# A second key buffer, level-one products in four array quarters, modulation sums without a total, and half the forward spectra

## The reference

```python
mod = silu(c) @ ada_w[layer] + ada_b[layer]              # shift, scale, gate rows
# RWKV-7, 16 heads of 64, context then latent tokens, both directions z
k_dir = k * (1 + (a - 1) * k_a);  b = kk * a             # a = sigmoid(a0 + low rank)
S = S * w_t + (S @ a_t) b_t^T + v_t k_t^T;  y_t = S @ r_t
# Hyena, order 2
z = x1 * fft_conv(v, kern[0]);  y = x2 * fft_conv(z, kern[1])
# experts: top-1 group, top-2 experts of 32
y_e = (silu(x @ w_gate[e]) * (x @ w_up[e])) @ w_down[e]
```

## Time and profile before

| | |
|---|---|
| median of 3 runs | 1964.73 us (1961.82 to 1973.62) |
| profiled execution | 1960.14 us |
| its span in the trace | 1958.2 us |
| mean granted clock of TensorE | 0.969 |
| PE, PEld, DVE, ACT, POOL busy | 1776.7, 941.9, 773.4, 531.2, 52.1 us |
| chain steps, first to last copy of U | 149.8 to 702.9 us |
| convolutions | 1355.7 us to about 1450 us |

### The profile page before, as it was taken

One profiled execution on the slowest core, in us unless ns is written; L12 is line 12 of the kernel. 1 busy time (PEld: TensorE's weight loads), 2 busy tenths in 40 slices (PEclk: granted clock), 3 DMA queues, 4 the chain that ended last, 5 costly groups with the idle time before them and its releaser, 6 DMA issues. The chain is left out here.

```text
span 1958.2 us, 34257 instructions
## 1 busy us (share of the span) xinstructions
PE 1776.7 (91%) x13979; PEld 941.9 (48%) x13979; DVE 773.4 (39%) x1910; ACT 531.2 (27%) x993; POOL 52.1 (3%) x45
## 2 busy tenths in 40 slices
PE   5788898898897888999999999898999999999996
PEld 2344555555555544443443443675654444444442
DVE  5766677777777335200100101564735110110101
ACT  3244454554454321111111111213321111111111
POOL 0010000000100000000000001000000000000001
PEclk8989899999999899999999999999999999999998
DMA  9013323323323468999999997232166999999993
GB/s 308 26 33 101 99 73 114 114 77 111 110 76 127 162 238 360 427 428 428 428 429 428 428 416 277 76 128 112 82 272 272 427 428 428 428 428 428 428 413 123
DMA packets 105168, 504.05 MB, mean 257 GB/s; under 512 B 15568, under 2 KB 60352, under 8 KB 79184
## 3 DMA queue, kind: packets, MB, share of 16 engines
q1 hardware_dynamic: 103728, 501.88, 64.4%
q10 hardware_dynamic: 1312, 0.37, 0.1%
HBM read 501.13 MB, written 1.09 MB: 256 GB/s over the span
## 5 line engine op out<-in xcount | busy, mean ns | idle before, releaser
L2009 DVE TENSOR_TENSOR arena<-banks,arena 128x512 f32<-128x512 f32 x32 | 22.1, 692 | 660.5 <-PE banks L1821 660.5
L1821 PE MATMUL banks<-arena 128*64 128x512 f32 x1024 | 226.4, 594 | 10.5 <-DMA arena<-in_moe_w_up 10.5
L1843 PE MATMUL banks<-arena 128*64 128x512 f32 x1024 | 226.8, 596 | 3.3 <-ACT arena L1940 3.3
L1812 PE MATMUL banks<-arena 128*64 128x512 f32 x1024 | 225.3, 593 | 3.3 <-DVE arena L1932 3.3
L775 PE MATMUL banks<-arena 128*128 128x512 f32 (+1 forms) x384 | 159.3, 553 | 0.8 <-ACT arena L1086 0.8
L1821 PEld LDWEIGHTS banks<-arena 128*64 128x64 f32 x1024 | 82.1, 137 | 152.8 <-issue 152.8
L1812 PEld LDWEIGHTS banks<-arena 128*64 128x64 f32 x1024 | 74.2, 137 | 147.8 <-issue 144.2
L1843 PEld LDWEIGHTS banks<-arena 128*64 128x64 f32 x1024 | 70.7, 137 | 154.4 <-issue 150.7
L1934 ACT ACTIVATE arena<-banks,arena 128x128 f32<-128x128 f32 x128 | 48.1, 456 | 335.5 <-PE banks L1801 335.5
L1801 PEld LDWEIGHTS banks<-arena 128*128 128x128 f32 x1024 | 118.4, 194 | 28.1 <-issue 24.3
L1801 PE MATMUL banks<-arena 128*128 128x128 f32 x1024 | 124.5, 281 | 3.5 <-DVE arena L2004 3.5
(11 more groups left out here) (394 smaller groups left out, 2398.0 us busy)
## 6 DMA issues: line engine op xcount, KB each, us to landing
arena<-in_moe_w_gate SPq DMA_DIRECT2D x64, 2048.0 KB, 14.9
arena<-in_moe_w_up SPq DMA_DIRECT2D x64, 2048.0 KB, 17.1
arena<-in_moe_w_down SPq DMA_DIRECT2D x64, 2048.0 KB, 12.8
arena<-in_ada_w SPq DMA_DIRECT2D x128, 192.0 KB, 2.9
...
```

Source lines behind the costliest of these rows:

```text
L1812: mm = pe.matmul(G[j * CAP:(j + 1) * CAP, :], xT[:, t, j * CAP:(j + 1) * CAP], wg[par][j][:, t], start=(t == 0), stop=(t == KT - 1))
L1821: mm = pe.matmul(U[j * CAP:(j + 1) * CAP, :], xT[:, t, j * CAP:(j + 1) * CAP], wu[j][:, t], start=(t == 0), stop=(t == KT - 1))
L1843: mm = pe.matmul(bank[j * CAP:(j + 1) * CAP, :], hT[:, t, j * CAP:(j + 1) * CAP], wd[j][:, t, half * 512:(half + 1) * 512], start=(t == 0) ...
L2009: dve.tensor_tensor(h, U[:, :], sg, ALU.mult).then_inc(h_ready, 1)
```

## The change

Seven things change.

1. There are two key buffers, KK[n % 2]. key_rates, key_products and rates of group q = m + 2 move to slots 20, 22 and 23 of the round before, the sum and the features are spread over slots 0, 1, 3 and 4, and products_early goes from slot 6 to 5, kept_early from 7 to 6. factors is cut into inner_factors (slot 21 of the round before) and outer_factors (z = 0 in slot 22 of the round before, z = 1 in slot 1).
2. level_one makes both results together, in four quarters: for each block s1 in its own partition half and s2 in the other (z swapped); level_two_z and level_two follow with the half of z2 and s2 exchanged.
3. The modulation's four weight tiles are summed in PSUM. Each product is made in four column groups of a quarter of the piece's width, so 16 products stand in place of four; the total, its copy and ACT's store go. DVE's second sum writes the row, on four partitions, and SP stores it ahead of the next bias. The modulation's places in open_order and the slots change (h0 in slot 2, h1 in 7; the products a after h4, the products w in slot 14).
4. A pair of low rank products takes both banks before the first product.
5. sum_directions alternates between its two outputs.
6. ACT does a Sigmoid on one spare word in slot 11, and decay_rank moves to slot 14.
7. In the convolutions only the first block of each forward spectrum's matrix is used: the products of even and odd tokens are kept apart, ACT copies one of them, and DVE makes sum and difference as the two blocks.

The diff, cut:

```diff
+    def part(self, piece):
+
+        return self.width(piece) // 4
+
+    def store(self, sp, m, piece, open_dve):
+
+        layer, cols = self.place(m, piece)
+        sp.wait_ge(open_dve, OPEN.taken(m, f"h{2 * piece + 1}")[1])
+        sp.dma_start(self.mods[layer, 0, cols].rearrange("(g n) -> g n", g=4),
+                     self.row[0:P:32, 0:self.part(piece)]).then_inc(self.row_out, 16)
...
-            if half == 0:
-                sp.wait_ge(open_dve, OPEN.taken(*before)[1])
         if half == 0:
-            sp.dma_start(self.bias[0:1, 0:self.width(piece)], self.ins["ada_b"][layer, cols].unsqueeze(0)).then_inc(self.bias_in, 16)
+            if m or k:
+                self.store(sp, *((m, piece - 1) if piece else (m - 1, self.PIECES - 1)), open_dve)
+            sp.dma_start(self.bias[0:P:32, 0:self.part(piece)],
+                         self.ins["ada_b"][layer, cols].rearrange("(g n) -> g n", g=4)).then_inc(self.bias_in, 16)
...
-        for g in range(self.HALF):
-            mm = pe.matmul(bank[g * 32:(g + 1) * 32, 0:self.width(piece)], self.cond[:, half * self.HALF + g],
-                           self.w[g][:, 0:self.width(piece)], start=True, stop=True, tile_position=(0, g * 32))
+        n = self.part(piece)
+        for t in range(self.HALF):
+            for g in range(4):
+                mm = pe.matmul(bank[g * 32:(g + 1) * 32, 0:n], self.cond[:, half * self.HALF + t],
+                               self.w[t][:, g * n:(g + 1) * n], start=(t == 0), stop=(t == self.HALF - 1), tile_position=(0, g * 32))
         return mm
...
-        order += [(m, u) for u in ("wy0", "wy1", "h0") if chain]
-        order += [(m, u) for u in ("h1", "t0") if chain]
+        order += [(m, u) for u in ("h0", "wy0", "wy1") if chain]
+        order += [(m, u) for u in ("h1",) if chain]
         order += [(m + 1, u) for u in ("v",) if now]
         order += [(m, u) for u in ("h2",) if chain]
         order += [(m + 1, u) for u in ("bc", "kc", "vc") if now]
         order += [(m - 1, u) for u in ("rows",) if behind]
-        order += [(m + 2, u) for u in ("w0", "w1") if early]
+        order += [(m + 1, u) for u in ("wyc",) if now]
         order += [(m, u) for u in ("h3",) if chain]
-        order += [(m + 1, u) for u in ("wyc",) if now]
-        order += [(m, u) for u in ("t1",) if chain]
-        order += [(m + 2, u) for u in ("k", "a0", "a1") if early]
+        order += [(m + 2, u) for u in ("w0", "w1", "k") if early]
         order += [(m, u) for u in ("h4",) if chain]
+        order += [(m + 2, u) for u in ("a0", "a1") if early]
         order += [(m + 2, u) for u in ("norm",) if early]
         order += [(m, u) for u in ("h5",) if chain]
         order += [(m + 2, u) for u in ("rg",) if early]
-        order += [(m, u) for u in ("t2",) if chain]
...
-    BB, KK = [s.take(STEPS, 2, C) for _ in range(2)], s.take(STEPS, 2, C)
+    BB, KK = [s.take(STEPS, 2, C) for _ in range(2)], [s.take(STEPS, 2, C) for _ in range(2)]
...
-                    if slot == 2 and 0 <= n and n + 1 < CH:
+                    if slot == 4 and 0 <= n and n + 1 < CH:
                         sp.wait_ge(open_done, OPEN.done(n, "rg"))
                         r.load_first(sp, ins, n + 1)
                     if slot == 13 and 0 <= n and n + 1 < CH:
                         sp.wait_ge(open_done, OPEN.done(n, "v"))
                         r.load_values(sp, ins, n + 1)
-                    if 0 <= m < CH and slot in (4, 8, 12, 15, 19):
-                        later.load(sp, m, (4, 8, 12, 15, 19).index(slot) + 1, open_done, open_dve)
+                    if 0 <= m < CH and slot in (3, 8, 12, 15, 19):
...
-                if name == "w0":
+                if name == "w":
                     pe.wait_ge(kr_in, 96 * (n + 1))
-                z = int(name[1])
-                w, x = (w2, r.wl) if name[0] == "w" else (a2, r.al)
-                pe.matmul(open_bank(n, name)[:, :], w[rows(z), :], x[rows(z), :], start=True, stop=True).then_inc(open_done, 1)
+                w, x = (w2, r.wl) if name == "w" else (a2, r.al)
+                banks = [open_bank(n, f"{name}{z}") for z in range(2)]
+                for z in range(2):
+                    pe.matmul(banks[z][:, :], w[rows(z), :], x[rows(z), :], start=True, stop=True).then_inc(open_done, 1)
...
-                level(n, "s1" + "cl"[half], lambda z, b: S2[:, half, b], lambda z, b: z1[:, b])
-                level(n, "s2" + "cl"[half], lambda z, b: z1[:, b], lambda z, b: S2[:, half, b])
+                first, second = (inverse_bank(n, k + "cl"[half]) for k in ("s1", "s2"))
+                for b in range(BLK):
+                    at = slice(b * C, (b + 1) * C)
+                    s2_, z_ = S2[:, half, b], z1[:, b]
+                    pe.matmul(first[rows(0), at], s2_[rows(0)], z_[rows(0)], start=True, stop=True)
+                    pe.matmul(second[rows(0), at], z_[rows(1)], s2_[rows(1)], start=True, stop=True)
+                    last_first = pe.matmul(first[rows(1), at], s2_[rows(1)], z_[rows(1)], start=True, stop=True)
+                    last_second = pe.matmul(second[rows(1), at], z_[rows(0)], s2_[rows(0)], start=True, stop=True)
+                last_first.then_inc(inv_done, 1)
+                last_second.then_inc(inv_done, 1)
...
                     if chain and slot == 2:
                         level_one_z(m, 1)
+                        modulate(m, 0)
                         from_values_late(m, 0)
                     if chain and slot == 3:
                         from_values_late(m, 1)
-                        modulate(m, 0)
                     if chain and slot == 4:
                         level_one(m, 1)
+                    if now and slot == 5:
+                        products_early(n)
                     if chain and slot == 6:
+                        level_two_z(m, 1)
+                    if chain and slot == 7:
                         modulate(m, 1)
-                    if now and slot == 6:
-                        products_early(n)
-                    if chain and slot == 7:
-                        level_two_z(m, 1)
                     if now and 7 <= slot < 9:
                         products_late(n, slot - 7)
                     if chain and slot == 8:
-                        total(m, 0)
                         level_two(m, 1)
                     if now and 9 <= slot < 12:
                         project(n, "v", ((0, 1, 2), (3, 4, 5), (6, 7))[slot - 9])
                         modulate(m, 2)
                     if now and slot == 12:
                         turn(n, "bc", BB[n % 2], 0)
-                        turn(n, "kc", KK, 0)
+                        turn(n, "kc", KK[n % 2], 0)
                     if now and slot == 13:
                         turn(n, "vc", VV, 0)
                     if behind and slot == 13:
                         out_rows(m - 1)
-                    if early and slot == 13:
-                        low_rank(q, "w0")
-                        low_rank(q, "w1")
+                    if now and slot == 14:
+                        from_values_early(n)
                     if chain and slot == 14:
                         modulate(m, 3)
-                    if now and slot == 14:
-                        from_values_early(n)
-                    if chain and slot == 15:
-                        total(m, 1)
+                    if early and slot == 14:
+                        low_rank(q, "w")
                     if early and 15 <= slot < 18:
                         project(q, "k", ((0, 1), (2, 3, 4), (5, 6, 7))[slot - 15])
-                    if early and slot == 18:
-                        low_rank(q, "a0")
-                        low_rank(q, "a1")
                     if now and slot == 18:
                         level_one_z(n, 0)
                     if chain and slot == 18:
                         modulate(m, 4)
+                    if early and slot == 18:
+                        low_rank(q, "a")
...
-            def factors(n, z):
+            def inner_factors(n, z):
                 act.wait_ge(dec_ready, 2 * n + z + 1)
                 inner, sign = (sg[z], -1.0) if z == 0 else (cum[z], 1.0)
-                outer = cum[z] if z == 0 else sg[z]
+                act.activation(inner, inner, ACT.Exp, scale=sign * HALF_DECAY)
...
+            def outer_factors(n, z):
+                outer, sign = (cum[z], -1.0) if z == 0 else (sg[z], 1.0)
                 to = late(n % 2, z, 1)
+                if z == 0 and n >= 2:
+                    act.wait_ge(g_done, STEPS * (n - 1))
                 act.activation(to, outer[:, L:TOK].rearrange("p (j t) -> p j t", t=C), ACT.Exp, scale=sign * HALF_DECAY)
-                act.activation(inner, inner, ACT.Exp, scale=sign * HALF_DECAY)
                 act.drain()
                 act.activation(outer, outer, ACT.Exp, scale=-sign * HALF_DECAY)
...
-                    if now and slot == 1:
-                        factors(n, 0)
                     if chain and slot == 1:
```

(72 more changed lines are left out.)

97 lines of the change are left out of this document (43 added, 54 removed).

## The result

The changed kernel takes 1947.1 us (median of 6 runs, 1942.6 to 1950.0) beside 1966.5 us for the kernel before (6 runs in the same session, 1960.8 to 1973.6): a ratio of 0.990, with an interval of 0.988 to 0.992. The forecast was 1900, with a range from 1874 to 1934. The sign was right, the size was not: 1.0% came of 3.3%.

A forecast was written before the change was run, and what follows sets the result against it. The prediction took PE to lead the head rounds with DVE close behind, a chain of eight steps setting each round. Heads 54.5 us and convolutions 6 us off the profiled 1960.14 gave 1900, range 1874 to 1934.

The forecast's parts named there:

- Step 0: First to second copy of U in a round: 8.01 to 6.8 us, ACT's exponentials and the wait before L877 gone.
- Step 4: Fifth to sixth copy of U: 10.77 to 10.6 us, w products waiting 2.3 to 2.6 for the h3 sum.
- Step 5: Sixth to seventh copy of U: 10.80 to 10.1 us, a products 0.6 shorter but waiting 0.4 for h4.
- Step 3: Fourth to fifth copy of U: 8.21 to 8.3 us, with the sigmoid's table load ahead of the turned tiles' copies.
- Steps 1, 2, 6 and 7: Other steps between copies of U in a round: 5.4, 9.1, 7.2 and 8.1 us forecast.
- Level one: Two level-one results together in four quarters: 0.9 us less per pair, 16 pairs, 14.5 us.
- The modulation products and totals: Head rounds: totals removed save 2.4 us a round, 19 in all; modulation products in column groups cost PE no change.
- The third rival: Slower: short modulation products' weight loads do not overlap, 2.7 us more a group, 130 us, giving 2030; chance 0.04.
- The convolutions: Convolution stage: halved forward and inverse products against added DVE operations, 6 us saved.
- the fast side: Head rounds: PE stalls vanish rather than move, 24 us more saved over seven rounds, giving 1876; chance 0.12.
- a slow side: DVE becomes the bound wherever its work was moved, a saving of only 30 us, giving 1930; chance 0.17.
- 1900 and its surroundings: Whole kernel: the main forecast, 1884 to 1918 us; chance 0.62.

The follow-up runs named there:

- e1: The changed kernel with modulation product h0 put back behind both late value products, in bank order and slot 3: 1929.5 us, ratio 0.985.
- e2: The changed kernel with the low rank products of w and their sigmoids put back ahead of modulation product h3: 1933.1 us, ratio 0.986.
- e3: The changed kernel with both orders put back, h0 behind the late value products and w with its sigmoids ahead of h3: 1913.9 us, ratio 0.976.
- e10: The kernel before with only the modulation change: four column groups, no totals, store on SP; orders, slots and key buffer as before: 1948.4 us, ratio 0.994.
- e8: e3 with the two low rank products of the rates put ahead of modulation product h4, in bank order and on PE: 1917.4 us, ratio 0.977.
- e9: e3 without the early sigmoid on a spare word, so the table load stands later again: 1924.6 us, ratio 0.981.
- e5: The kernel before with only level one in four array quarters and the swapped halves in level two: 1963.8 us, ratio 1.0006.
- e4: e3 with level one written again as two levels of two quarters, one after the other: 1916.6 us, ratio 0.977.
- e6: The kernel before with only the convolution change, products of even and odd halves with sum and difference on DVE: 1962.0 us, ratio 1.0004.

## Why the forecast missed, point by point

By the profiled executions 60.5 us were to go and 16.9 went. Of the 43.6 missing, about 28.6 are in the first six rounds, 8.4 in the last two, 4.4 in the opening and 2.3 behind the rounds.

- **Step 0 (forecast 6.8, came 8.6).** This is a wait that was left out, not a mis-sized one. The forecast said that the wait before L877 goes and stopped there. It never asked who holds the bank of wy1 once h0 stands ahead in the ring. The diff shows the order; DVE's slot 3, level copy before `modulate(m, 0)`, was in the text of the kernel. e1 shows 2.0 us a round.
- **Step 4 (10.6, came 12.7).** The mechanism was named, the w products waiting for h3, and e2 shows it to be the cause. Its size was wrong: 2.3 to 2.6 us were laid out, 3.35 came, and the work behind it is slower as well. The low rank pair then takes 1.71 us in step 4, and four records of the same kind 1.1 in step 5. The windows view has the granted clock at 0.50 for 3.4 us behind the wait, at 0.62 over the pair, and at 1.00 in step 5:

```profile
402.70:406.10 3.40, 3.27 (x22) 1.34 (x19) 1.40 (x4) 1.42 (x3) 0.00 (x0) 0.50 0.31 80
402.30:404.00 1.70, 1.70 (x8) 0.36 (x11) 0.00 (x0) 0.56 (x2) 0.00 (x0) 0.62 0.06 11
416.60:417.70 1.10, 1.08 (x6) 0.34 (x6) 0.95 (x5) 0.00 (x0) 0.00 (x0) 1.00 0.35 102
```

  So the lower clock that follows the long wait adds 0.6 us to the pair and some 1.6 to the step, and the forecast's sum left it out: e3's step of 8.83 us has 1.58 of waits, its other 7.25 and the wait of 3.35 make 10.6, and this one took 12.2.
- **Step 5 (10.1, came 11.1).** The forecast had 0.4 us of wait for h4, and the changed kernel has 0.54. So the wait does not explain the miss, and e10 has 11.2 here without any moved bank use. What makes this step longer with the shorter modulation products was not found. In e3 the wait grows to about 1.1, since PE comes to it sooner; e8 shows that it is worth 1.0 us in this step and can't be had for nothing.
- **Step 3 (8.3, came 8.8).** The early table load costs 0.5, not 0.1, of step 3. e9 shows what it saves: 2.8 us of step 4 in e3's order. The edit that looks like a cost is one of the useful ones.
- **Steps 1, 2, 6 and 7 (29.8, came 29.8).** These hold in sum and nearly one by one: 5.4, 9.6, 6.6, 8.2 against 5.4, 9.1, 7.2, 8.1. Step 1 is partly luck: it would be 4.7, as in e1 and e3, without the "issue" waits, whose cause is open. The stall for DVE before the state product, 25.0 us in the earlier trace rows, is gone from the first six rounds, and the solve waits for DVE's sum in step 6 as forecast, 1.25 us for the 1.5 laid out.
- **Level one (14.5; by the medians nothing in e5, 3 in e4).** The price was right and the place was not. The 64 instructions run from 372.69 to 373.63 in the changed kernel, some 1.1 with the last one's end, 0.8 less than the 1.9 read from the earlier trace rows. But what PE waits for next ends later than either form: DVE's features in step 1 (0.41 against 1.17) and DVE's sum in step 6 (0.48 against 1.26). The forecast took 0.9 off two steps because PE leads the round; it did not look at what PE waits for next behind this group.
- **The modulation products and totals (19, came 14.4).** The price was right: 1536 instructions take 48.1 us, a group 1.08 at 128 columns and 0.80 to 0.87 at 96, in the changed kernel. Their lines:

```profile
L253 PE MATMUL banks<-arena 128*32 128x96 f32 (+1 forms) x1536 | 48.1, 265 | 9.0 <-DMA arena<-in_ada_w 5.3 <-issue 3.7
L253 PEld LDWEIGHTS banks<-arena 128*32 128x32 f32 x1536 | 36.0, 112 | 18.2 <-issue 15.9
```

  The 1536 loads of 112 ns cover 36.0 us, 23 ns apiece, as in the earlier trace rows. The third rival at 2030 is out. The rule of the Trainium skill (TensorE: Matmul & The Clock Gate, Part 3, The mechanism), by which these loads would not overlap, does not describe them. The Trainium skill (TensorEngine Tiling (Array Packing), Key Properties) has different tiles loading and multiplying at once, and with that this trace agrees, at 23 ns for a load of 112.
- **The moves around the second key buffer.** No term of the sum stood for them alone, and they turned out to be the largest part. From e10's 1948.4 to e4's 1916.6 lie 31.8 us; e4 has all of e3 but level one, so this is the moved work with both orders put back, with the low rank pairs, the early table load and about 3 us of convolutions in it. No run has the key buffer alone.
- **The rounds counted.** Seven rounds at the full saving and 3.5 us more for the last were laid out. Round 6 has no work for the next round but one, so fewer of the stalls that could go. The last two rounds took 112.7 us before and 110.3 after: 2.4 us for the forecast's 10.8. In e3 they give 7.3. This stretch varies by itself: it takes 114.4 us in e6, whose rounds are those of before, and 105 to 111 in the kernels with both orders put back. The first copy of U stands at 154.2 instead of 149.8, and at 152.8 in e5 and 154.3 in e10, so the opening, priced at nothing, cost about 4 us. Why was not tried.
- **The convolutions (6, came 3).** The layout on DVE was right. Counted from the stage's start, DVE's first products of the two halves come at 8.7 and 19.4 us, forecast 8.5 and 19.3. What came late is the end of each inverse, at 31.8 for 30.1 and at 61.9 for 58.6, 1.7 us an order. Of this the granted clock behind PE's wait is 1.25 and 1.41. The forecast had the wait and left out what follows it.

Put together: the steps that failed are the wait that the new place of h0 makes (step 0), the size of the wait for h3 with the low clock behind it (step 4), and the 14.5 us of level one taken off a PE that waits for DVE next. The round that the forecast described, 65.6 us, is what e3 runs, 65.5, but partly by chance. In e3 step 4 is 1.8 better than forecast and step 5 is 1.5 worse. The forecast described a kernel that the diff was not. The chances leaned too far as well: 0.12 stood on the fast side and 0.17 on a slow side that ended at 1930, and the case that the moved bank uses make new waits of 2 us in two steps was held within "1900 and its surroundings".

The clock was to lean to the fast side and did not. The windows view has 0.95 in the changed rounds, 0.96 before, 0.98 in e3's profile (0.96 in e4's). Executions of one kernel differ by as much (the kernel before has mean clocks of 0.964 to 0.973, with times of 1969 to 1956 us), so no part of the miss is charged to it but the 1.6 us of step 4 and the 1.3 us of each inverse, where the rows show it behind a wait.
